# Expert stage of a hybrid decoder step: the dot products read the token's row from SBUF instead of from a copy in PSUM

## The reference, cut to what matters

```
q = (xb @ w_q).reshape(TOK_BLK, PEER_HEADS, 2, DK_HALF)
s = einsum('thcd,hcnd->thcn', q, sub_keys)
s1, i1 = top_k(s[:, :, 0], TOPK);  s2, i2 = top_k(s[:, :, 1], TOPK)
cand = s1[..., :, None] + s2[..., None, :]
top_s, pos = top_k(cand, TOPK)
eid = take_along_axis(i1 * N_KEYS + i2, pos)
g = softmax(top_s)
hid = gelu(einsum('thkd,td->thk', u_tab[eid], xb))
y = einsum('thk,thkd->td', g * hid, v_tab[eid])
```

## Time and profile before

| What | us |
|---|---|
| Median of 3 runs | 2052.39 |
| Range of the runs | 2046.03 to 2052.77 |
| The profiled execution's own time | 2051.2 |
| Its span, first to last instruction | 2048.3 |
| Expert stage in it (first gather to the end) | 395.5 to 2048.3 |

### The profile page before, as it was taken

How to read it: one execution, slowest core, us unless ns; L and a number is a source line. 1 busy time by engine, 2 the same in 40 slices (tenths; PEclk the granted TensorE clock), 3 DMA queues, 4 the chain that set the end, 5 groups by cost and what they waited for, 6 DMA issues and landing times.

```text
span 2048.3 us, 19348 instructions
## 1 busy us (share of the span) xinstructions
PE 1625.9 (79%) x5414; PEld 745.2 (36%) x5414; DVE 1147.9 (56%) x3207; ACT 392.8 (19%) x1051; POOL 1057.8 (52%) x1168
## 2 busy tenths in 40 slices
PE   6999888978888877777777778777777777877677
PEld 3566454444443333333333333333322323322211
DVE  2220565467677777656555665666556555666641
ACT  2111443122221111111111211111121111111212
POOL 3000100145565565566666666666666666666663
PEclk9999899999999999999999999999999999999999
DMA  6110875588998898899999999999999999999996
GB/s 214 63 66 9 305 264 190 203 312 309 322 345 335 335 332 336 324 362 369 371 353 358 369 376 368 354 363 367 364 361 374 352 366 367 357 359 358 380 367 240
DMA packets 188136, 640.99 MB, mean 313 GB/s; under 512 B 19408, under 2 KB 35072, under 8 KB 187936
## 3 DMA queue, kind: packets, MB, share of 16 engines
q0 software_dynamic: 160640, 587.53, 77.0%
q1 hardware_dynamic: 27424, 52.60, 7.5%
HBM read 634.44 MB, written 5.60 MB: 312 GB/s over the span
## 4 chain that ended last, share of the span: by engine, by line
PE 34%; DMA 19%; POOL 16%; DVE 13%; issue 12%; another core or an unknown queue 3%; ACT 1%; DVEq 0%; SPq 0%; ACTq 0%; POOLq 0%
POOL area_r L1339 16%; PE bank L651 13%; DMA area_r<-in_v_tab,eid 11%; PE bank L474 8%; DMA area_r<-in_u_tab,eid 7%; PE bank L622 4%; DVE area_r L1223 4%; PE bank L593 3%; PE bank L564 1%; PE bank L412 1%; PE bank L517 1%; DMA area_w<-in_w_in 1%; PE bank L471 1%; DMA area_w<-in_v_cache 1%
## 5 line engine op out<-in xcount | busy, mean ns | idle before, releaser
L651 PE MATMUL bank<-area_r,area_c 128*128 128x512 f32 (+1 forms) x2176 | 1067.6, 623 | 348.8 <-DMA area_r<-in_v_tab,eid 282.6
L1223 DVE CUSTOM_DVE_ANT_0 area_r<-area_r,bank 128x1024 f32<-128x1024 f32 x544 | 640.4, 1218 | 308.5 <-DMA area_r<-in_u_tab,eid 284.8
L651 PEld LDWEIGHTS bank<-area_r,area_c 128*128 128x128 f32 (+1 forms) x2176 | 380.7, 190 | 965.7 <-issue 838.9
L1339 POOL DMA_INDIRECT area_r<-in_v_tab,eid x544 | 514.9, 947 | 399.8 <-PE bank L651 199.5
L1339 POOL DMA_INDIRECT area_r<-in_u_tab,eid x544 | 510.4, 938 | 288.3 <-issue 156.6
L877 ACT ACTIVATE area_c<-ident,wts 128x128 f32<-128x128 f32 (+1 forms) x544 | 197.5, 391 | 557.8 <-PE bank L651 266.4
L474 PE MATMUL bank<-area_w,area_t 128*128 128x384 f32 (+1 forms) x448 | 158.7, 510 | 7.5 <-DMA area_w<-in_w_in 5.9
L622 PE MATMUL bank<-area_w,area_t 128*128 128x256 f32 (+3 forms) x640 | 145.7, 381 | 3.2 <-ACT area_c L718 2.5
L622 PEld LDWEIGHTS bank<-area_w,area_t 128*128 128x128 f32 (+1 forms) x640 | 110.8, 175 | 47.0 <-issue 19.8
L474 PEld LDWEIGHTS bank<-area_w,area_t 128*128 128x128 f32 x448 | 84.4, 192 | 70.0 <-issue 17.5
L1317 POOL MEMSET area_x<- 128x192 f32 x2 | 0.5, 258 | 151.6 <-ACT area_r L718 151.6
(11 more groups left out here) (136 smaller groups left out, 1058.9 us busy)
## 6 DMA issues: line engine op xcount, KB each, us to landing
area_w<-in_k_cache SPq DMA_DIRECT2D x8, 1920.0 KB, 9.2
area_w<-in_v_cache POOLq DMA_DIRECT2D x8, 1920.0 KB, 9.1
area_w<-in_w_in SPq DMA_DIRECT2D x6, 1536.0 KB, 12.6
area_r<-in_u_tab,eid POOLq DMA_INDIRECT x544
area_r<-in_v_tab,eid POOLq DMA_INDIRECT x544
area_w<-in_w_q SPq DMA_DIRECT2D x8, 1024.0 KB, 10.6
area_x<-in_x_p SPq DMA_DIRECT2D x8, 512.0 KB, 8.9
area_w<-in_w_out SPq DMA_DIRECT2D x1, 4096.0 KB, 14.0
```

The lines of the kernel that those rows point to most:

```text
L651: mm = pe.matmul(acc[0:n, c, :], diag[s][:, 0:n], v_ring[s][:, c * 512:(c + 1) * 512], start=False, stop=False, skip_group_check=True)
L1223: vec.tensor_tensor_reduce(out=u_ring[s], in0=u_ring[s], in1=x_cur, scale=1.0, scalar=0.0, op0=ALU.mult, op1=ALU.add, accum_out=hid[:, j:j ...
L1339: nc.gpsimd.indirect_dma_start(out=ring[s], out_offset=None, in_=table, in_offset=bass.IndirectOffsetOnAxis(ap=eid[:, column:column + 1], ...
```

## The change

`x_cur` in PSUM is gone, and with it `set_x`. The dot products take the tile's rows from `xn` where they lie. For the sample tile `spread_samples` repeats the 32 rows on the four groups of partitions, into the SBUF room of the first tile's rows, which are no longer needed by then; it takes the place of the last `set_x`. At the start the semaphore that `set_x(0)` raised is raised by an instruction without work.

```
-        x_cur = wide(1, D)
+        x_rep = xn[:, 0, :]
...
-            def set_x(t):
-                if t < SAMP:
-                    ins = vec.tensor_copy(x_cur, xn[:, t, :])
-                else:
-                    for g in range(GROUPS):
-                        ins = vec.tensor_copy(x_cur[g * NSAMP:(g + 1) * NSAMP, :], xn[0:NSAMP, t, :])
+            def spread_samples():
+                for g in range(GROUPS):
+                    ins = vec.tensor_copy(x_rep[g * NSAMP:(g + 1) * NSAMP, :], xn[0:NSAMP, SAMP, :])
                 return ins
+
+            def x_of(g):
+                if isinstance(g, int):
+                    t = max(t for t in range(NT) if FIRST[t] <= g)
+                    return xn[:, t, :] if t < SAMP else x_rep
+                return xn[:, looped[0], :]
+
+            looped = [0]
...
-                    vec.tensor_tensor_reduce(out=u_ring[s], in0=u_ring[s], in1=x_cur, scale=1.0, scalar=0.0,
+                    vec.tensor_tensor_reduce(out=u_ring[s], in0=u_ring[s], in1=x_of(g), scale=1.0, scalar=0.0,
                                              op0=ALU.mult, op1=ALU.add, accum_out=hid[:, j:j + 1]).then_inc(u_free, 1)
...
-                if next_tile is not None:
-                    then(set_x(next_tile))
+                if next_tile == SAMP:
+                    then(spread_samples())
...
-            set_x(0).then_inc(u_free, UR)
+            dve.sem_inc(u_free, UR)
...
             for t in range(NT):
                 loop, rest = steps_of(t)
+                looped[0] = t
```

## The result

The changed kernel takes 2103.38 us (median of 4 runs, 2091.85 to 2110.79) where the kernel before, on the same chip, takes 2049.21 us (median of 4, 2044.06 to 2052.77): a ratio of 1.0261, 95% interval 1.0207 to 1.0316. It is slower, by 54 us. The prediction was 2135 us with a range of 2068 to 2210: right in sign and range, 32 us too high. The profiled execution took 2104.25 us, 53 more than that of before.

The account below looks back on a forecast made before the run. The expert stage was taken as a loop through POOL, transfers, DVE and PE that no engine fills. From 2051.2 us, +72 (24 one-head steps), +7, +5, -1 and +1 gave 2135 us, range 2068 to 2210.

Parts of the forecast that it names:

- The wait itself: POOL's gathers, reading indices from SBUF, wait for a two-SBUF-input DVE operation's end and finish 0.82 us after it.
- Its size in a step: Time added to POOL's gathers per one-head step: burst 4.7 us plus single dot products 3.5 us, together 8.2 us.
- The cover: What hides added gather time per step: last three dot products 1.5, middle pause 2.7, less queueing 1.0 us.
- B: POOL's pause in the middle of a step, waiting for a free v slot; its 2.7 us were to cover longer gathers.
- One of the signs: Expected trace evidence: gather line's median above 937 ns, POOL busy up some 250 us, 2.28 us spacing, GB/s below 350.
- (c): Rival: the reduce form reads its second input differently, so no contention; only the copies are left, 2050 us; chance 0.10.
- The first tile: Seven two-head steps, where POOL's 7.1 us pause for DVE takes up most: +1 us each, +7 us.
- The last steps: Last two steps, without routing and with hardly a burst, one still gathering u: +5 us.
- The copies: PSUM copies at tile ends go, four SBUF copies return, while DVE waits for u rows later: -1 us, bound -10.
- (a): Rival: memory sets the pace, so all 6.1 us of pauses cover; 1.1 us a step remain, 2084 us; chance 0.22.
- (b): Rival: nothing is covered, both pauses stay and all 32 gathers shift, 8.2 us a step, 2260 us; chance 0.12.
- (d): Rival: faster, no contention and DVE's tile-end work on the path, -9.8 us for the copies, 2041 us; chance 0.04.

Follow-up runs that it names:

- e5: Kernel before with its 544 v gathers replaced by plain DMAs of the same size, without indices, issued by POOL: 1886.62 us, one run.
- e6: Changed kernel with its 544 v gathers replaced by plain DMAs of the same size, without indices, issued by POOL: 1899.08 us, one run.
- e10: The changed kernel itself, run again on a fourth chip against the kernel before there: 2106.18 us, ratio 1.0329.
- e7: Kernel before without the copies at tile ends, all tiles using the first tile's row in PSUM: 2048.76 us, ratio 1.0002.
- e2: Kernel before, with only the dot products of the second to fourth tile reading rows from SBUF: 2115.58 us, ratio 1.0313.
- e12: Kernel before with two short memsets on POOL ahead of each gather, dot products still reading PSUM: 2045.34 us, ratio 1.0047.
- e1: Kernel before, with only the first tile's dot products reading rows from SBUF and the first copy gone: 2045.6 us, ratio 0.9958.
- e11: Kernel before with only the first tile's dot products reading SBUF, first copy gone, repeated on a fourth chip: 2034.06 us, ratio 0.999.
- e8: Kernel before with one single-column memset on POOL ahead of each v gather, on another chip: 1899.88 us, ratio 1.0021.
- e9: Kernel before with one memset on POOL ahead of each u and v gather, on another chip: 1908.19 us, ratio 1.0084.

## Why the prediction was right, and where it was off

- **The wait itself** held as it was read from two chance meetings in the earlier trace rows: 0.82 us after the end of the DVE operation was said, 0.81 measured; let in between dot products, 2.28 us apart in a burst, 2.3 measured; read of the indices, borne out by e5 and e6. The Trainium skill, "SBUF — State Buffer", section "SBUF: two separate sides", has GpSimd unable to write descriptors beside a VectorE operation in a two-port performance mode, but lets one with two SBUF inputs hold up only a GpSimd operation that reads SBUF. The traces agree with the second: the plain DMAs of e6 took 581 ns, the gathers between them 1206. By the sentence of the Trainium skill, "Perfetto Trace Analysis", section on SWDGE, that such DMAs read no tensor, neither kind would have waited; the u gathers with their indices did.
- **Its size in a step**: 8.2 us was said, 6.7 measured (6.2 in the step shown). The burst was mis-sized: nine dot products and 4.5 gathers were said to give 4.7 us. In the step shown six come back to back, and 0.75 + 1.05 + 1.04 = 2.8 us are added; in the mean of steps 8 to 28 it is 7.2 dot products and 3.3 us. As I read it, gathers that are late in one burst leave fewer landed rows for the next. The single dot products came to 3.4 us there, 3.3 in the mean, where 3.5 was said, but that is luck: seven at 0.5 us were said, and it is ten at 0.34 in the step shown (8.8 at 0.37 in the mean).
- **The cover**: 5.2 us was said, 3.7 measured (pauses of 6.6 us a step down to 2.9). B with 2.7 came off in full. The three last dot products were said to give 1.5 and gave 1.0. The 1.0 us less of queueing never came: from the last u gather to its dot product lie 6.1 us in both kernels. This step of the working was wrong. Together +2.9 us a step instead of +3.0: two errors, of 1.5 us each, that cancel. That the net term came out so close is luck; the wait, its place beside the dot products and the cover by pause B were right.
- **One of the signs failed.** Line 1345's median was to rise above 937 ns; it is 937 ns for u gathers and 940 for v. Only 308 of 1088 gathers are over 1.1 us, most of the others as short as before. The same median would have spoken for (c). The other signs held: the mean, 224 us more busy time (250 said), starts 2.3 us apart in a burst, B gone, 343 GB/s.
- **The first tile** was said to lose 7 us and gained 6.5: from the first gather to the first v gather of step 7 the profile has 393.8 us, 400.3 before. POOL's pauses took up the longer gathers, as the prediction had it, but more of them went than was added (see below).
- **The last steps** were said to cost 5 us; from step 31 to the end it is +0.3. And 8.3 us of the profile's difference stand ahead of all dot products: the first gather came at 387.2 us instead of 395.5. That isn't shown to come from the change: in e10, the same kernel, it came at 399.5, and in all other profiles between 392.6 and 400.1. So the spans differ by 23 x 2.92 = 67.1 for steps 8 to 30, 1.3 for step 7, 0.3, -6.5 and -8.3: 53.9 us. Of the forecast's 84 us, 13.5 too many are the first tile, 3.6 the one-head steps, 4.7 the last ones, and 8.3 the start. Of these the start is likely chance. In e10 the changed kernel lost 70 us against its own kernel before, nearer to the forecast.
- **The dot product** at +2 ns was +7 (1225 against 1218), beside waits, as said. The rule cited from the Trainium skill, "VectorE: DVE Perf Modes", by which it would be 65 ns shorter, does not agree with the trace for this form either.
- **The copies** at -1 us were nothing, by e7, whose interval reaches 4 to 5 us either way.
- **The rivals.** (a), all cover used and 1.1 us a step, falls: 2.9 us of pause remain in each step and it grew by 2.9. But it was nearer than (b), which had nothing covered: 3.7 of 6.7 us are. (c), no contention in the reduce form, falls with the first gather of a burst. (d), faster, falls for the whole; the small thing in its favour, a first tile that gains, came by another road than the copies.

## What to carry to other kernels

Before an operand is moved from PSUM to SBUF "to save a copy", count how many SBUF inputs the DVE instruction then has, and ask what POOL does at that time: an indirect DMA that must read indices waits for the end of a DVE instruction with two of them (here 0.94 us became up to 2.01), while a plain DMA does not (581 ns against 570). A chance meeting in the old trace (one gather of 1.75 us beside one of 0.94) prices this before anything is built. What it costs in the end is not the sum of the waits, but what of them lies on POOL's own stretch of the loop, less the pauses there: 6.7 us added gave 2.9, while 5.5 us spread evenly gave 1.

## What was not expected

- **The first tile is faster with longer gathers.** From the first gather to step 7 it takes 400.3 us before, 397.5 in e7 and 401.6 in e2, whose first tile is that of the kernel before; 390 to 394 in the six profiles in which its dot products read SBUF in whole or in part; and 379.4 in e12, where the gathers are only wider apart. DVE's waits in the window 440 to 850 us, first of the kernel before, then of the changed one, show u rows on time in the one and late in the other, and the changed one still ends sooner:

```profile
DVE area_r L1223 <- DMA area_r<-in_u_tab,eid: 23.8, 17, 1.9
...
DVE rtu L1138 <- remote: 11.0, 4, 3.0
```

```profile
DVE area_r L1228 <- DMA area_r<-in_u_tab,eid: 65.6, 36, 3.4
```

  All waits of DVE named "remote" there add up to 29.7 us before, 29.3 in e7 and 29.0 in e2, but 8.2 after and 0 in e1, e11 and e12. I take it that late signals go with gathers that follow each other closely, and that wider spacing ends them. This is argued from those sums, not shown: no run changed the first tile's spacing alone. Nor does it make a faster kernel by itself: the time of e11 is that of its kernel before.
- **Chips differ more than the change.** The kernel before takes 2049 to 2053 us on two chips, 2036 on a third and 1893 on a fourth (e8 and e9), where a window of e8 moves 400 GB/s at a DMA share of 1.01 (363 and 0.97 before), and a step takes 42.2 us. In e8 the first part of a step has no pause B at all (0.03 us). By the accounting above the change would have no cover there and cost more than 5 us a step; the changed kernel wasn't run on that chip.
